# Decay sums of a state-space stage built level by level instead of by prefix scans

## What is computed

```python
log_f = jnp.logaddexp(jnp.log(lb), jnp.log1p(-lb) + jax.nn.log_sigmoid(hf32))
k_in = -jnp.expm1(log_f)
# S_t = diag(f_t) S_{t-1} + k_t v_t^T,   o_t = S_t^T q_t
```

## Time and profile before

| | us |
|---|---|
| median of 3 runs (2407.68 to 2413.14) | 2412.85 |
| the profiled execution, its own time | 2402.32 |
| its span in the trace | 2400.5 |
| PE busy with matmuls | 2292.5 |
| DVE busy | 1046.7 |
| ACT busy | 609.2 |
| POOL busy | 1463.4 |
| mean granted TensorE clock | 0.987 |

### The profile page before, as it was taken

One profiled execution on the slowest core, in us unless ns is written; L12 is line 12 of the kernel. 1 busy time (PEld: TensorE's weight loads), 2 busy tenths in 40 slices (PEclk: granted clock), 3 DMA queues, 4 the chain that ended last, 5 costly groups with the idle time before them and its releaser, 6 DMA issues.

```text
span 2400.5 us, 30516 instructions
## 1 busy us (share of the span) xinstructions
PE 2292.5 (96%) x10971; PEld 1837.0 (77%) x10971; DVE 1046.7 (44%) x1623; ACT 609.2 (25%) x1060; POOL 1463.4 (61%) x1452
## 2 busy tenths in 40 slices
PE   5999999999999999998999999999998779999999
PEld 4676788788888896667878888888885437888887
DVE  7685763542331147759635323211482552322300
ACT  3323323321110023243242211110333452211100
POOL 5554655776766755546648766667582216766663
PEclk9999999999999999999999999999999999999999
DMA  3321232522222233212334222323321002233332
GB/s 144 104 79 53 84 93 84 162 97 97 96 96 97 97 104 106 71 59 83 92 110 142 97 96 96 96 93 98 122 98 44 1 0 71 92 98 98 96 98 79
DMA packets 68628, 217.35 MB, mean 91 GB/s; under 512 B 8368, under 2 KB 8496, under 8 KB 68400
## 3 DMA queue, kind: packets, MB, share of 16 engines
q1 hardware_dynamic: 52640, 187.72, 24.4%
q10 hardware_dynamic: 15888, 28.21, 3.3%
HBM read 195.93 MB, written 10.49 MB: 86 GB/s over the span
## 4 chain that ended last, share of the span: by engine, by line
PE 88%; DVE 5%; ACT 4%; issue 1%; POOL 1%; DMA 1%; ACTq 0%; SPq 0%; POOLq 0%; DVEq 0%
PE ps L1549 77%; PE ps L1834 2%; PE ps L1998 2%; ACT pe L946 2%; DVE small L1221 1%; PE ps L1740 1%; PE ps L1780 1%; DVE b_sb L1399 1%; PE ps L1765 1%; PE ps L2047 1%; PE ps L1721 1%; PE ps L1793 1%; PE ps L1877 1%; DMA w_raw<-wst 1%; PE ps L2055 1%
## 5 line engine op out<-in xcount | busy, mean ns | idle before, releaser
L511 POOL TENSOR_TENSOR w_lo<-w_raw,w_hi 128x512 fp32r<-128x512 f32 x700 | 945.9, 1351 | 58.4
L508 POOL TENSOR_SCALAR w_hi<-w_raw 128x512 fp32r<-128x512 f32 x700 | 496.5, 709 | 717.9 <-DMA w_raw<-wst 675.2
L1549 PE MATMUL ps<-h_hi,w_lo 128*128 128x512 f32 (+1 forms) x2048 | 805.8, 393 | 34.9 <-POOL w_lo L511 8.9
L1549 PE MATMUL ps<-h_hi,w_hi 128*128 128x512 f32 (+1 forms) x2048 | 786.9, 384 | 0.0
L1549 PE MATMUL ps<-h_lo,w_hi 128*128 128x512 f32 (+1 forms) x2048 | 786.9, 384 | 0.0
L1549 PEld LDWEIGHTS ps<-h_hi,w_lo 128*128 128x128 f32 x2048 | 388.4, 190 | 140.6 <-issue 37.3
L1549 PEld LDWEIGHTS ps<-h_lo,w_hi 128*128 128x128 f32 x2048 | 388.1, 190 | 78.1 <-issue 6.2
L1549 PEld LDWEIGHTS ps<-h_hi,w_hi 128*128 128x128 f32 x2048 | 388.2, 190 | 76.4
L1549 PE MATMUL ps<-a_hi,w_lo 128*128 128x512 f32 (+1 forms) x572 | 213.7, 374 | 0.0
L1549 PE MATMUL ps<-a_hi,w_hi 128*128 128x512 f32 (+1 forms) x572 | 213.2, 373 | 0.0
L1549 PE MATMUL ps<-a_lo,w_hi 128*128 128x512 f32 (+1 forms) x572 | 213.2, 373 | 0.0
(11 more groups left out here) (278 smaller groups left out, 2598.7 us busy)
## 6 DMA issues: line engine op xcount, KB each, us to landing
w_raw<-wst SPq DMA_DIRECT2D x350, 512.0 KB, 3.5
rot<-raw ACTq DMA_DIRECT2D x70, 128.0 KB, 2.1
gates<-gt ACTq DMA_DIRECT2D x32, 256.0 KB, 4.1
stage<-gates ACTq DMA_DIRECT2D x32, 256.0 KB, 3.1
x_sb<-xin SPq DMA_DIRECT2D x4, 512.0 KB, 7.9
out<-x_sb SPq DMA_DIRECT2D x8, 256.0 KB, 4.4
kc<-cst ACTq DMA_DIRECT2D x1, 1056.0 KB, 4.9
kc<-cst ACTq DMA_DIRECT2D x1, 481.0 KB, 5.0
```

What stands on the lines that cost most here:

```text
L508: eng.tensor_scalar(w_hi[s][:, part], w_raw[s][:, part], 1.0, 1.0, ALU.mult, ALU.mult)\
L511: eng.tensor_tensor(w_lo[s][:, part], w_raw[s][:, part], w_hi[s][:, part].bitcast(F32), ALU.subtract)\
L1549: m = eng.matmul(o, w, x, start=first and i == 0, stop=final and i == 2)
```

## The change

The log decay is written to `b_sb` itself, and no scan is run. `b_sb` then holds, at every stage, sums that start at the beginning of each segment of w tokens, and exponent(j) doubles the segment first: it adds the left half's total to the right half (one instruction of 1024 columns, in place, followed by a wait of DVE for its own result). Only the left half of x is then computed by a subtraction; the right half's exponent is what `b_sb` holds there, and ACT exponentiates it from `b_sb` straight into x. So `decay(1)` to `decay(7)` are two instructions of 1024 columns each in place of one with 2048. exponent(1) has one instruction where it had two, exponent(2) to exponent(7) have two as before, exponent(8) has one where it had none. The keys' scaling and `keys_ready` now stand behind exponent(1), and the exponential of the block totals stands in `decay(8)`.

```diff
@@ ACT
                 def decay(j):
-                    if j == 8:
+                    eng.wait_ge(lvd, 9 * l + j)
+                    if j <= LEVELS:
+                        w = 1 << (j - 1)
+                        xa, xb = (xf[j % 2].rearrange("p (n s w) -> p n s w", s=2, w=w)[:, :, i, :] for i in range(2))
+                        bb = bl.rearrange("p (n s w) -> p n s w", s=2, w=w)[:, :, 1, :]
+                        step(eng.activation(xa, xa, ACT.Exp))
+                        eng.activation(xb, bb, ACT.Exp).then_inc(lve, 1)
+                    elif j == 8:
                         eng.wait_ge(lv_mm, 8 * l + 7)
                         eng.activation(xf[0], bl, ACT.Exp).then_inc(lve, 1)
-                        return
-                    eng.wait_ge(lvd, 8 * l + min(j, 8))
-                    eng.activation(xf[j % 2], xf[j % 2], ACT.Exp).then_inc(lve, 1)
+                        totals = b_sb[:, :, :].rearrange("p h (n t) -> p (h n) t", t=P)[:, :, P - 1]
+                        eng.activation(small[:, 96:112], totals, ACT.Exp).then_inc(et_ready, 1)
+                    else:
+                        eng.activation(xf[1], xf[1], ACT.Exp).then_inc(lve, 1)
...
                 decay(1)
 
-                small_b = b_sb[:, :, :].rearrange("p h (n t) -> p (h n) t", t=P)[:, :, P - 1]
-                eng.activation(small[:, 96:112], small_b, ACT.Exp).then_inc(et_ready, 1)
                 gate_step(0)
@@ DVE
                     after(k)
-                    k = step(eng.tensor_tensor(xf[0], bf, xf[1], ALU.subtract))
+                    k = step(eng.tensor_tensor(bf, bf, xf[1], ALU.subtract))
                 else:
-                    k = step(eng.tensor_scalar(xf[0], xf[1], -1.0, None, ALU.mult))
+                    k = step(eng.tensor_scalar(bf, xf[1], -1.0, None, ALU.mult))
                 eng.tensor_tensor(fl, fl, xf[1], ALU.add).then_inc(prep_v, 1)
                 after(k)
-                for h in range(HH):
-                    for t in range(TB):
-                        cols = slice(t * P, (t + 1) * P)
-                        kb = step(eng.tensor_tensor_scan(b_sb[:, h, cols], ones, xl[0][:, h, cols], 0.0,
-                                                         ALU.mult, ALU.add))
-                eng.wait_ge(prep_a, 3 * l + 3)
-                if l:
-                    for h in range(HH):
-                        kb = step(eng.tensor_scalar(f_sb[:, h, :], f_sb[:, h, :], lbv[5][:, h:h + 1], None,
-                                                    ALU.mult))
-                eng.tensor_copy(small[:, 112:113], small[:, 126:127]).then_inc(keys_ready, 1)
-                after(kb)
-                eng.wait_ge(hq_ready, l + 1)
...
                 def exponent(j):
                     x = xf[j % 2]
                     if j >= 2:
                         eng.wait_ge(lv_mm, 8 * l + j - 1)
+                    if 2 <= j <= LEVELS + 1:
+                        w = 1 << (j - 2)
+                        ba, bb = halves(bf, j - 1)
+                        whole = ba[:, :, w - 1:w].to_broadcast(list(ba.shape))
+                        if j == LEVELS + 1:
+                            eng.tensor_tensor(bb, bb, whole, ALU.add).then_inc(lvd, 1)
+                        else:
+                            after(step(eng.tensor_tensor(bb, bb, whole, ALU.add)))
                     if j <= LEVELS:
                         w = 1 << (j - 1)
-                        (xa, xb), (ba, bb) = halves(x, j), halves(bf, j)
-                        ref = ba[:, :, w - 1:w].to_broadcast(list(ba.shape))
-                        step(eng.tensor_tensor(xa, ref, ba, ALU.subtract))
-                        eng.tensor_tensor(xb, bb, ref, ALU.subtract).then_inc(lvd, 1)
+                        ba = halves(bf, j)[0]
+                        whole = ba[:, :, w - 1:w].to_broadcast(list(ba.shape))
+                        eng.tensor_tensor(halves(x, j)[0], whole, ba, ALU.subtract).then_inc(lvd, 1)
                     elif j == 9:
+                        eng.wait_ge(lvd, 9 * l + 8)
...
+                eng.wait_ge(prep_v, 2 * l + 2)
                 exponent(1)
+                eng.wait_ge(prep_a, 3 * l + 3)
+                if l:
+                    for h in range(HH):
+                        k = step(eng.tensor_scalar(f_sb[:, h, :], f_sb[:, h, :], lbv[5][:, h:h + 1], None, ALU.mult))
+                    after(k)
+                eng.tensor_copy(small[:, 112:113], small[:, 126:127]).then_inc(keys_ready, 1)
+                eng.wait_ge(hq_ready, l + 1)
                 weigh(1)
```

## The result

| | kernel before | changed kernel | ratio, 95% interval |
|---|---|---|---|
| first comparison, medians | 2408.61 (8 runs) | 2395.02 (8 runs) | 0.9946 [0.993, 0.9962] |
| second | 2407.17 (17 runs) | 2398.58 (7 runs) | 0.9965 [0.9954, 0.9976] |
| third | 2405.93 (24 runs) | 2397.29 (7 runs) | 0.9953 [0.9935, 0.9971] |

The ratio is not the quotient of the two medians (which is 0.9964 for the third comparison). The changed kernel is faster by 8 to 14 us. The first comparison's 2395.02 lies 1.5 under the range of the prediction (2396.5 to 2411.5). The profiled execution took 2395.83, span 2393.9, against 2402.32 and 2400.5 before.

A forecast was written before the change was run, and what follows sets the result against it. PE was taken as the bound (88% of the chain), with gains only up to level 1. 7.3 us in layer 1 plus 0.64 in layer 0, clock nothing, made 7.9 off 2412.85: 2404.9, range 2396.5 to 2411.5.

The forecast's parts named there:

- my sum: Layer 1, DVE and ACT steps from exponent(1) to level 0's copy: level 1 at 1118.6 instead of 1125.90, 7.3 earlier.
- 4.87 and 1.05: Layer 1, PE's waits for keys_ready before level 0 (4.87) and for gate 0's copy before gate 2 (1.05): both gone.
- The cover of the later costs: Rounds from level 2 on: DVE's added wait (0.12) and ACT's longer pair (0.2) cost zero within 0.6 a round, 6.4 total.
- rival 3: Level 1's strided exponentials on ACT take 4.0 a pair, clock falls in layer 1: 0.8 slower, 2413.7; chance 0.07.
- the waits of layer 0: Layer 0 before level 1: decay(1) starts 0.95 earlier, level 1 comes 0.64 earlier, PE's idle falls from 2.60 to 1.96.
- the clock at nothing: Low clock behind the idles before level 1: one fall expected, as in the trace of before, so it adds nothing.
- two coins, the middle is one fall: Idles of 1.96 and 2.1 before level 1 may each drop the clock or not; one fall taken, 4.9 each.
- the base: The gain of 7.9 was taken from the median 2412.85, 10.5 above the profiled execution of 2402.32.

The follow-up runs named there:

- the loaded rounds: Changed kernel with two dead multiplications of 1024 columns more on DVE in each of five rounds per layer: 0.9991 of the kernel before, median 2402.61.
- the early keys': Kernel before with the keys' scaling and keys_ready moved between the 8th and 9th scan in layer 1: 0.9988, median 2405.84.
- with scans: Changed kernel with the 16 scans put back as dead work: both layers 0.9989, layer 0 only 0.9966, layer 1 only 0.9984.

## Why the prediction was right and wrong

**Right.** In layer 1 level 1 stood 7.3 earlier in my sum. From the start of gate 0 to level 1 it was 29.5 (1096.4 to 1125.90) and is 21.7 (1090.0 to 1111.66), 7.8 earlier. That 4.87 and 1.05 would vanish, that level 1 would still wait for the copy of level 0 (2.1 in my sum, 1.60 in the trace), that ACT would set the start of weigh(1) through its table load, and that the rounds stay PE's at 9.06: all are in the profile after. The cover of the later costs, 0.6 a round and 6.4 in total, was enough; the loaded rounds show one at least as large. The keys' scaling, 2.00 in the sum, took 4.22, but off the chain that level 1 waits for. The strided exponentials cost 0.1 more each and not twice, so rival 3 is out. With it goes, for a stride of two, what the Trainium skill's rule on adjacent pairs (Vector Engine (DVE) Microarchitecture Reference, "Measured stream behaviour on trn2") would have cost, 1.7 to 2.5 ns a column. If that rule is applied to ACT, the trace disagrees with it: 1.15 for 1024 columns is 1.12 ns a column.

**Wrong: the waits of layer 0.** The forecast had level 1 only 0.64 earlier there and PE's idle before it at 1.96, close to the 2.02 after which the clock had fallen. Level 1 is 1.5 earlier (22.7 after gate 0's start then, 21.2 now), and the idle is 1.15. Two terms were mis-sized. DVE in layer 0, first before, then after:

```profile
282.46 1.63 DVE L1424 TENSOR_TENSOR xl<-b_sb 128x1024 f32<-128x1024 f32 x1
284.02 2.31 DVE L1425 TENSOR_TENSOR xl<-b_sb 128x1024 f32<-128x1024 f32 x1
...
278.73 1.34 DVE L1440 TENSOR_TENSOR xl<-xl,f_sb 128x1024 f32<-128x1024 f32 x1 [8.44 <-ACT xl L816]
280.00 1.63 DVE L1441 TENSOR_TENSOR xl<-xl,hq_sb 128x1024 f32<-128x1024 f32 x1
282.15 1.70 DVE L1422 TENSOR_TENSOR b_sb<-b_sb 128x1024 f32<-128x1024 f32 x1 [0.53 <-PE ps L1840]
283.88 1.52 DVE L1427 TENSOR_TENSOR xl<-b_sb 128x1024 f32<-128x1024 f32 x1
```

I took weigh(1) at 1.52 + 2.29 and it took 1.34 + 1.63, where POOL's splits fell differently beside it (that these are the reason is argued, not shown); and exponent(2) took 1.70 + 1.52, where I had the old 1.63 + 2.31 plus a wait. Between the two DVE idled 0.53 for level 0 itself, a wait that my sum did not have. In both layers together level 1 is 9.2 to 9.3 earlier in the three profiles, where the forecast had 7.9.

**Right by luck: the clock at nothing.** From an idle of 1.96 and one of 2.1 I made "two coins, the middle is one fall", as before, and so let the clock add nothing. The count over the profiles is different. With the kernel before's idle of 2.6 in layer 0 the clock fell in 2 of 2 profiles (its own and the early keys'). With the 1.1 to 1.2 that the changed kernel has there, also with scans or loaded rounds, it fell in 3 of 7. In layer 1, with 1.6 to 1.7, it fell in 5 of 5, where the kernel before with 1.52 had no such fall. So the change takes about half of one fall away in layer 0 and adds one in layer 1: more falls than the forecast's one, but most of them shorter. From the start of level 1 to the start of level 2, both layers together, the kernel before took 23.0 and the changed kernel 21.5, 23.1 and 24.7, in the mean 23.1. So the clock added nothing in the mean, but in single profiles it gave 1.5 or took 1.8, and the zero is not made up as in my sum.

By the stage numbers the gain is 7.5 to 10.8 and not 7.9 alone, and its mean over the three profiles, 9.2, agrees with the second and third comparison (8.6 and 8.6 in the medians, 0.35% and 0.47%). Up to 1 us more lies between level 2 of layer 0 and gate 0 of layer 1; I did not look for its cause.

**Wrong: the base.** The forecast was set against the median of 3 runs, 2412.85. Without this step the measured time, 1.5 under the range, would have lain inside it. The same kernel's medians over 8, 13, 17, 24 and 29 runs are 2408.61, 2405.99, 2407.17, 2405.93 and 2406.22. Of the 9.9 us between 2404.9 and 2395.02, 4.2 are the base, 1.4 are the waits by the stage's traces, and the other 4.3 are open. Set against 2408.61, the same sum gives 2400.7, and the range, moved with it, 2392.3 to 2407.3. I had noted that the profiled execution was 10.5 under the median and allowed only 1.9 for it at the low end; the single runs of the kernel before spread over 2395.0 to 2415.11.

**Open.** Why the first comparison gave 13.6 us and the other two 8.6 is not settled. The intervals overlap, and the third block, with clock falls at other places in each profile, varies by 5.8 (702.8 to 708.6) over the fourteen profiles; that this is the cause is argued, not shown.

## What to carry to other kernels

The largest wait in a profile is not what its removal is worth: follow the chain of the engine that is late to the last thing it must deliver, and first ask whether that thing stands behind work that nobody waits for yet. Here moving one copy ahead of one exponent gave as much as deleting all scans, and both together 20 us. Where PE idles before a stretch of small matmuls, as here 1.1 to 2.9 us before level 1, count the low clock behind it (here 3.2 to 4.9) as part of the wait. And set a forecast of a third of a per cent against many runs of the kernel before, not three.

## What the runs showed of the hardware

The same idle time of 1.1 to 1.2 before the same instruction was followed by a fall of the granted clock from 2.4 to 1.2 GHz in 3 profiles and by none in 4, so single executions of one kernel differ from one such place alone: the changed kernel's layer 0 by 3.2 (30.3 and 33.5). The fall came around the start of level 1, in some profiles 1 to 2 us behind it, after which the clock stood at 1.2 GHz for 6.8 to 10.2 us. Once it had come, full speed did not come back within the level in any profile; at level 0 of layer 1, with 128 columns a matmul, it did (0.50 for 3 to 4 us in the four profiles that had it, then 1.00). Exponentials at a stride of two fp32 words, or in runs of two, took 1.13 to 1.17 for 1024 columns, in longer runs 1.04 to 1.09. `copy_predicated` with runs of one or two words took 2.5 where it took 1.3 with longer runs, in every kernel.
